# Value products of two pairs in every second turn, for query blocks 2 and 3

## The reference, cut to what matters

```
s_c = q @ kc * scale + bias_c ;  p_c = masked_softmax(s_c, rel_c >= 0)  ;  o_c = p_c @ vc
s_s = q @ k_sel * scale + bias_s ;  p_s = masked_softmax(...)           ;  o_s = p_s @ v_sel
s_w = q @ kwb * scale + bias_w ;  p_w = masked_softmax(...)             ;  o_w = p_w @ vwb
o = gb[..., 0:1] * o_c + gb[..., 1:2] * o_s + gb[..., 2:3] * o_w
```

## Time and profile before

| | |
|---|---|
| median of three runs | 1054.36 us (1054.12 to 1054.89) |
| span of the profiled execution | 1050.5 us (3.9 us less than that median: what lies around the span) |
| TensorE busy | 1038.4 us (99%) |
| VectorE busy | 593.9 us (57%) |
| ScalarE busy | 445.9 us (42%) |
| granted TensorE clock, mean | 0.999 of full |

### The profile page before, as it was taken

One profiled execution on the slowest core, in us unless ns is written; L12 is line 12 of the kernel. 1 busy time (PEld: TensorE's weight loads), 2 busy tenths in 40 slices (PEclk: granted clock), 3 DMA queues, 4 the chain that ended last, 5 costly groups with the idle time before them and its releaser, 6 DMA issues.

```text
span 1050.5 us, 13952 instructions
## 1 busy us (share of the span) xinstructions
PE 1038.4 (99%) x5453; PEld 846.1 (81%) x5453; DVE 593.9 (57%) x1110; ACT 445.9 (42%) x855; POOL 51.0 (5%) x71
## 2 busy tenths in 40 slices
PE   9999999999999999999999999999999999999997
PEld 7877778888888888888888888899888677777785
DVE  6466665445356666533466563553456673567757
ACT  5355542233345434431234442453244454556640
POOL 0000000000001100000000000125200001000000
PEclk9999999999999999999999999999999999999999
DMA  7421133222341842333122323334211222511012
GB/s 277 160 65 57 61 101 100 95 89 98 123 140 41 275 152 87 98 125 110 61 101 85 100 97 110 131 122 135 91 61 61 61 81 71 211 41 41 21 61 80
DMA packets 29106, 107.08 MB, mean 102 GB/s; under 512 B 3227, under 2 KB 3371, under 8 KB 28401
## 3 DMA queue, kind: packets, MB, share of 16 engines
q1 hardware_dynamic: 24864, 86.13, 24.8%
q0 software_dynamic: 4032, 19.96, 5.3%
q10 hardware_dynamic: 144, 0.10, 0.0%
HBM read 101.44 MB, written 7.36 MB: 104 GB/s over the span
## 4 chain that ended last, share of the span: by engine, by line
PE 88%; DVE 5%; ACT 4%; issue 2%; DMA 2%; DVEq 0%; SPq 0%; ACTq 0%
PE ps L780 26%; PE ps L782 25%; PE ps L781 25%; PE ps L1054 2%; PE ps L1222 2%; PE ps L1205 1%; PE ps L1187 1%; DMA raw<-wp 1%; ACT whi L1285 1%; PE ps L1143 1%; PE ps L1106 1%; ACT SC L1336 1%; PE ps L1175 1%; DVE wlo L1633 0%; DVE SC L1739 0%
## 5 line engine op out<-in xcount | busy, mean ns | idle before, releaser
L780 PE MATMUL ps<-XH,whi 128*128 128x512 f32 (+1 forms) x864 | 336.7, 390 | 0.6 <-DVE XL L1646 0.2
L782 PE MATMUL ps<-XH,wlo 128*128 128x512 f32 (+1 forms) x864 | 326.9, 378 | 0.0
L781 PE MATMUL ps<-XL,whi 128*128 128x512 f32 (+1 forms) x864 | 326.5, 378 | 0.0
L1633 DVE TENSOR_TENSOR wlo<-raw,whi 128x1024 fp32r<-128x1024 f32 (+1 forms) x158 | 191.6, 1218 | 166.7 <-ACT whi L1285 166.1
L1285 ACT CAST whi<-raw 128x1024 fp32r<-128x1024 f32 (+1 forms) x158 | 161.2, 1027 | 95.9 <-PE ps L782 70.5
L780 PEld LDWEIGHTS ps<-XH,whi 128*128 128x128 f32 x864 | 162.6, 188 | 43.0 <-issue 12.4
L782 PEld LDWEIGHTS ps<-XH,wlo 128*128 128x128 f32 x864 | 162.6, 188 | 31.2
L781 PEld LDWEIGHTS ps<-XL,whi 128*128 128x128 f32 x864 | 162.8, 188 | 27.8 <-issue 0.5
L780 PE MATMUL ps<-whi,GH 128*128 128x512 f32 x176 | 68.8, 391 | 0.0
L782 PE MATMUL ps<-whi,GL 128*128 128x512 f32 x176 | 68.5, 389 | 0.0
L781 PE MATMUL ps<-wlo,GH 128*128 128x512 f32 x176 | 68.5, 389 | 0.0
(11 more groups left out here) (305 smaller groups left out, 1333.1 us busy)
## 6 DMA issues: line engine op xcount, KB each, us to landing
raw<-wp SPq DMA_DIRECT2D x150, 512.0 KB, 3.5
vec_dram<-row_dram POOLq DMA_DIRECT2D x1, 3072.0 KB, 13.7
H<-x POOLq DMA_DIRECT2D x1, 2048.0 KB, 8.1
x_dram<-H POOLq DMA_DIRECT2D x1, 2048.0 KB, 8.8
A<-w1c POOLq DMA_DIRECT2D x2, 1024.0 KB, 6.3
A<-x_dram POOLq DMA_DIRECT2D x1, 2048.0 KB, 12.8
y<-A SPq DMA_DIRECT2D x8, 256.0 KB, 2.0
raw<-wp SPq DMA_DIRECT2D x4, 402.0 KB, 3.9
```

Of the source, the lines that this page charges most:

```text
L780: self.e.matmul(o, ah, bh, start=start, stop=False)
L781: self.e.matmul(o, ah, bl, start=False, stop=False)
L782: return self.e.matmul(o, al, bh, start=False, stop=stop)
L1633: self.e.tensor_tensor(wlo[BUF[i]][:, 0:w], raw[i % NR][:, 0:w], whi[BUF[i]][:, 0:w].bitcast(F), ALU.subtract).then_inc(sems["lo"], 1)
```

## The change

PV of pairs at places 0, 2, 4 and 6 of query blocks 2 and 3 is not issued in its own turn but together with PV of the next pair, one turn later. Place 8 stays alone. Eight pairs move: 18, 20, 22, 24, 27, 29, 31 and 33.

```diff
@@ -537,6 +537,9 @@
                 yield
             for s in turned:
                 en.n_tr(s)
+            if len(summed) == 1 and summed[0] > 17:
+                place = summed[0] % 9
+                summed = [] if place % 2 == 0 and place < 8 else summed if place == 8 else [summed[0] - 1, summed[0]]
             for s in summed:
                 en.n_pv(s)
             for s in scaled:
```

## The result

| | before | changed |
|---|---|---|
| median | 1054.24 us (4 runs, 1053.81 to 1054.89) | 1060.1 us (4 runs, 1059.18 to 1061.91) |
| ratio | | 1.0063, 95% interval 1.005 to 1.0075: slower by 5.3 to 7.9 us |
| span of the profiled execution | 1050.5 us | 1058.5 us |

The forecast was 1059.4 us, in a range of 1056.8 to 1061.8. The two profiled executions differ by 8.0 us, more than the medians: QK after turn 20, ahead of the first moved instruction, starts at 946.58 before and 947.33 now, so 0.75 of it was there already. One of the later executions of the changed kernel (experiment 5) took 1154.38 us at a mean granted clock of 0.849 and is left out of its ratio. From here on I use one measure for all kernels: the stretch from this QK (of pair 21) to the first matmul of the last product. Before, it is 1005.08 - 946.58 = 58.50 us; in the changed kernel 1013.06 - 947.33 = 65.73, +7.2.

What follows compares the result with a forecast made beforehand. TensorE, busy 99% of the span, was taken as the bound. Waits 4.35 plus tail 2.4 less 1.6 saved gave 5.15, taken as 5.0 on a 1050.5 span, plus 3.9: 1059.4 us, range 1056.8 to 1061.8.

Steps and rivals of the forecast that it cites:

- The waits: Turns 22 to 34: reduces of a pair wait for the moved PV, so the next QK stalls; 4.35 us in all.
- The single stall of turn 20: Before the change, the reduce of 31 keys waits for PV of its own turn; used to price the other stalls.
- The tail: Turn 35 to the last product: reduces, exponentials, copies and scaling hold up the last transposes; 2.4 us of wait.
- T: End of PV of 31 in turn 35, from which the times up to the last product were counted.
- The saved blocks: Joined PV and transposes start fewer blocks: 1.26 us from seven moved pairs, 0.37 at the end, together 1.6.
- a PV that comes right behind another PV should lose it: In the joined turns, the second PV drops the 0.18 us that comes once for each block.
- The clock: Rival: TensorE's gaps bring it to 1.2 GHz from turn 31 on, up to 20 us more, 1079 us; chance 0.03.
- one of the signs that I had named for a wrong forecast: In these turns: TensorE idle under 3 us, double PV costing twice the single one, or the clock leaving 1.00.
- the sum of 5.15: Whole kernel: 4.35 us of waits plus 2.4 at the end less 1.6 saved; 5.0 was taken, laying out turns gave 4.9.
- 3.9 us between its span and the median: Whole kernel: median of runs above the profiled span before, assumed untouched and added to 1055.5 us.
- only the blocks count: Rival: reduces find their slot free in time, so time falls by the 1.6 us saved, to 1052.8; chance 0.04.
- balanced waits: Rival: stalls are short and offset the blocks saved, within 2 us of before, about 1055.5 us; chance 0.09.

Runs made afterwards that it cites:

- experiment 5: The changed kernel unedited, run again, with two further profiled executions: 1060.3 us, ratio 1.0063 to the kernel before; the two single executions 1063.24 and 1061.8 us.
- experiment 2: Changed kernel with a fifth pair of slots for probabilities and a later load of the last norm's rows: 1052.52 us, ratio 0.9989 to the kernel before.
- experiment 6: Changed kernel with only pairs 31 and 33 delayed: 1056.33 us, ratio 1.0028 to the kernel before.
- experiment 3: Changed kernel, four pairs of slots, with PV of two pairs put behind QK of their turn, ahead of second-lane matmuls and transposes: 1053.83 us, ratio 1.0004.
- experiment 7: Kernel before, without the change, given the fifth pair of slots and later load of the last norm's rows: 1052.43 us, ratio 0.999.
- experiment 8: Changed kernel with five pairs of slots and only PV of one kind joined: 1052.91 us, ratio 0.9989 to the kernel before.
- experiments 1: Changed kernel without its last two delayed pairs, 31 and 33: 1056.81 us, ratio 1.0039 to the kernel before.
- experiment 4: Changed kernel with five matmuls of 128x512 added in TensorE's gap ahead of the transposes of 34: 1060.49 us, ratio 1.0066.

## Why the prediction came out right

**The waits: right in place and size.** Here the turns of the changed kernel's profile against those of experiment 2, which has the same order without the wait. A turn is from QK to QK; 0.07 is added for the longer QK behind a wait, which the same turn's difference doesn't hold (it falls into the next turn; turn 34 has that of turn 33 in place of its own).

| turn | changed | five slots | wait | forecast |
|---|---|---|---|---|
| 22 | 4.15 | 3.10 | 1.12 | 1.01 |
| 24 | 4.59 | 4.13 | 0.53 | 0.56 |
| 26 | 5.02 | 4.43 | 0.66 | 0.56 |
| 28 | 4.14 | 4.14 | 0 | 0 |
| 31 | 4.62 | 3.32 | 1.37 | 1.29 |
| 33 | 5.27 | 4.78 | 0.56 | 0.63 |
| 34 | 3.54 | 3.38 | 0.16 | 0.3 |

The sum is 4.4, the forecast 4.35. The single stall of turn 20, with a reduce of 31 keys, did give the frame for all the others; its latency from PV to the reduce was short (0.03), in the others it is 0.13 (952.85 to 952.98 in turn 22).

**The tail: right within 0.3, by another last link.** The length was right, one link of the chain was not. From QK of 35 to the last product experiment 6 takes 1009.28 - 996.69 = 12.59, experiment 2 takes 10.01: 2.6 us, the forecast was 2.4. I had the transposes of 35 wait for the copies of 34, to end at T + 5.1. In experiment 6 (T is 1001.09) the scaling of 35 ends the wait, behind a second-lane subtraction that waits for the cast on ScalarE, and they end at 1006.51, T + 5.4. The link left out is that subtraction, 0.56.

**The saved blocks: half the size.** 0.86 in place of 1.6. The step that failed is "a PV that comes right behind another PV should lose it". It holds only for two PV of one kind. Pairs 20 and 29 are of 31 keys and their partners are not, and they save nothing; a join of two alike saves 0.14 to 0.16, not 0.18, as the double PV already said where I read it (1.90 against 2 x 1.02, 0.14). That makes 0.74 for the seven joins in place of 1.26. In the tail of experiment 2 the joined transposes take 1.98 and the three PV 2.77, 4.75 in place of 4.96: 0.21 where I had 0.37. These make 0.95, of which the stretch shows 0.86.

**The clock: a rival that I held out of the sum, and that is there in small.** All four profiles of the unedited change have a stretch at the lower level between 946 us and the last product. None of the five kernels without these waits has one there (before and experiments 2, 3, 7 and 8, one profile each), nor have experiments 1 and 6, with a part of the waits, or 4, with all of them in the turns. It costs the difference of the stretches to the one at full clock, 65.73 to 66.18 against 64.62, 1.1 to 1.6 us. My rival had the clock stay low from turn 31 to the last product for up to 20 us; it was back after 3.4 us in each of the four (the granted clock in windows of 0.5 us). But the clock leaving 1.00 was one of the signs that I had named for a wrong forecast, and it did; the sum has no term for it. Why one execution has it behind the gap of turn 31 and another behind that of the tail, and experiments 1 and 4 not at all behind the same gap of turn 31, nor experiment 6 behind that of the tail, stays open. By the rule of the Trainium skill that I named (TensorE: Matmul & The Clock Gate, Part 1: idleness brings the throttle back, activity releases it) the trace agrees in the direction.

**The sum as measured**: 4.4 + 2.6 - 0.9 = +6.1, which is experiment 4's stretch (64.62 - 58.50 = 6.1), and 1.1 to 1.6 of clock in the profiled executions. The forecast of 5.0 was low by the 0.7 of the blocks, 0.2 of the tail, the 0.15 between the sum of 5.15 and the 5.0 that I took, and by the clock, and the median (+5.9, by the ratio +6.6) is in the range. That it lies well inside is in part luck: the profiled stretches grew by 7.2 to 7.7, and the upper edge of the range was +7.4 (1061.8 - 1054.36). Why the medians grew by less isn't shown; one of the first four executions, that of 1059.18 us, has a mean clock of 0.999, as the profile of before has, where the others have 0.995 to 0.997, so the fall may not be in every execution. That the base had 3.9 us between its span and the median was an accident of its one execution: the changed kernel's profiled execution took 1060.14 us with a span of 1058.5, 1.6 more. It does no harm to the forecast of the difference.

The other rivals: "only the blocks count" is refuted by the result and by experiments 1 and 6; "balanced waits" too, since TensorE stood idle for 1.04 us ahead of QK of 23 and 1.30 us ahead of QK of 32.

## What to carry to other kernels

Where a buffer is used again after a fixed number of steps, moving its reader back by one step moves the writer's start by a whole step's work, and here both the writer's engine and the one that feeds it are on the path. Look for the wait in the code that releases the buffer, find one place in the trace where that wait already ends last, and price the others with it. A step that is moved within the turn, or one more buffer, avoids the wait; here only the buffer also kept the saving: the kernels with a fifth pair of slots took 0.9989 (with the change) and 0.999 (without) of the time before.

## What the runs showed of the hardware that I had not expected

- A block of matmuls whose stationary tile has another shape than the one ahead (128*64 behind 31*64, 128*64 behind 128*128) starts 0.14 to 0.18 us late; two blocks of PV alike in a row do so once. Two blocks of transposes joined save less, 0.06 us (1.98 in place of 2 x 1.02). A change from 31 rows to 128 costs as much as one from transposes to PV.
- One of the gaps of 1.3 us on a TensorE that is otherwise busy was followed by 3.4 us at 1.2 GHz in four profiles out of four of one kernel, at 0.43 in place of 0.23 us a matmul of 512 columns, while in one profile each of three kernels with some of the same gaps the clock stayed at 1.00.
- In 740 to 890 us, ahead of all that the kernels here change, the mean clock was 1.00 in the profiles of before, the changed kernel and experiments 1, 2 and 5, 0.99 in those of 3, 4, 6, 7 and 8, and 0.98 and 0.99 in the two further profiles of the change. Differences of 0.1% could be read from stretches of the trace, not from the medians alone, since executions of one kernel lie up to 4 us apart (18 of the kernel before, 1051.77 to 1055.71 us).
